# Upper and lower parts of 32 sample rows side by side as one 64-column stationary tile

## The reference

```python
h = rmsnorm(x, g_norm)
p = h @ w_in                                  # 1024 x 1408
u, v, xb, q = ...                             # 384, 384, 384 and 256 columns
a_out = gelu(u) * (causal W_s @ rmsnorm(gelu(v), g_v) + b_s)    # chunked spatial gate
b_out = pooled means of xb minus xb, a linear map per group, times a scale
x_out = attention of q into the memory keys and values
x = x + concat(rmsnorm of a_out, b_out, x_out) @ w_out
```

## Time and profile before

| what | value |
|---|---|
| median of 3 runs | 1500.94 us (1499.5 to 1501.42) |
| the profiled execution | 1504.31 us |
| its span, first to last instruction | 1502.6 us |
| PE busy | 1455.8 us, 97% of the span |
| DVE, ACT, POOL busy | 1175.2, 952.2, 112.2 us |
| HBM traffic | 303 GB/s over the span |
| mean granted TensorE clock | 0.991 of full speed |

### The profile page before, as it was taken

The page is one execution under the profiler, slowest core; times in us unless marked ns, Lnnn a source line. Parts: engine busy times, 40 slices in busy tenths (PEclk is TensorE's granted clock), DMA queues, the critical chain, the costliest instruction groups (busy, mean ns, idle before and its releaser), DMA issues.

```text
span 1502.6 us, 21721 instructions
## 1 busy us (share of the span) xinstructions
PE 1455.8 (97%) x7712; PEld 1239.2 (82%) x7712; DVE 1175.2 (78%) x1113; ACT 952.2 (63%) x914; POOL 112.2 (7%) x132
## 2 busy tenths in 40 slices
PE   7998999999999999999999999999999999999996
PEld 5888999999888778888888888888888887888774
DVE  6546776645546588888888888888888888889996
ACT  7535433344444667777777777777777776777773
POOL 1211311002122200000000000000000000001021
PEclk9999999999999899999999999999999999999998
DMA  9524687655422699999999999999999999999991
GB/s 376 224 91 150 228 273 273 238 180 185 174 86 85 245 367 362 360 395 363 357 390 365 364 383 378 369 367 384 369 353 395 370 360 356 362 371 362 390 384 64
DMA packets 67282, 456.32 MB, mean 304 GB/s; under 512 B 7636, under 2 KB 7930, under 8 KB 15639
## 3 DMA queue, kind: packets, MB, share of 16 engines
q1 hardware_dynamic: 59543, 427.91, 75.1%
q0 software_dynamic: 5680, 20.49, 3.5%
q10 hardware_dynamic: 2016, 7.34, 1.2%
HBM read 434.10 MB, written 21.88 MB: 303 GB/s over the span
## 4 chain that ended last, share of the span: by engine, by line
PE 89%; ACT 3%; DVE 3%; issue 2%; ACTq 0%; POOL 0%; DMA 0%; DVEq 0%; POOLq 0%; SPq 0%
PE bank L321 28%; PE bank L323 28%; PE bank L322 28%; ACT whi L305 2%; PE bank L1800 2%; DVE wlo L309 1%; ACT junk L537 1%; DVE x L1220 1%; PE bank L1553 0%; PE bank L1778 0%; DVE stage L1008 0%; PE bank L1755 0%; ACTq L776 0%; DMA stage<-in_mem 0%; DVE hT_lo L859 0%
## 5 line engine op out<-in xcount | busy, mean ns | idle before, releaser
L309 DVE TENSOR_TENSOR wlo<-raw,whi 128x2048 fp32r<-128x2048 f32 x401 | 918.6, 2291 | 187.8 <-ACT whi L305 186.6
L305 ACT ACTIVATE whi<-raw 128x2048 fp32r<-128x2048 f32 x401 | 767.1, 1914 | 155.4 <-PE bank L323 154.5
L321 PE MATMUL bank<-whi,gT_hi 128*128 128x512 f32 x896 | 364.8, 407 | 3.3 <-DVE gT_lo L1225 3.3
L323 PE MATMUL bank<-whi,gT_lo 128*128 128x512 f32 x896 | 355.5, 397 | 0.0
L322 PE MATMUL bank<-wlo,gT_hi 128*128 128x512 f32 x896 | 354.3, 395 | 0.0
L323 PEld LDWEIGHTS bank<-whi,gT_lo 128*128 128x128 f32 x896 | 169.3, 189 | 39.6
L321 PEld LDWEIGHTS bank<-whi,gT_hi 128*128 128x128 f32 x896 | 169.9, 190 | 37.6 <-issue 3.5
L322 PEld LDWEIGHTS bank<-wlo,gT_hi 128*128 128x128 f32 x896 | 170.1, 190 | 34.7
L321 PE MATMUL bank<-whi,eT_hi 128*128 128x512 f32 x448 | 177.4, 396 | 1.9 <-DVE eT_lo L1240 1.9
L322 PE MATMUL bank<-wlo,eT_hi 128*128 128x512 f32 x448 | 177.1, 395 | 0.0
L323 PE MATMUL bank<-whi,eT_lo 128*128 128x512 f32 x448 | 176.2, 393 | 0.0
(11 more groups left out here) (253 smaller groups left out, 1476.1 us busy)
## 6 DMA issues: line engine op xcount, KB each, us to landing
raw<-in_stream SPq DMA_DIRECT2D x402, 1024.0 KB, 5.6
x_slots<-zero POOLq DMA_DIRECT2D x18, 640.0 KB, 6.4
rows_e<-x_slots ACTq DMA_DIRECT2D x7, 512.0 KB, 7.5
y_slots<-y_rows ACTq DMA_DIRECT2D x7, 512.0 KB, 6.2
const<-in_const SPq DMA_DIRECT2D x1, 1192.0 KB, 21.7
stage<-in_mem SPq DMA_DIRECT2D x2, 512.0 KB, 4.3
xn<-in_x_prompt SPq DMA_DIRECT2D x1, 1024.0 KB, 11.0
out_y_prompt<-xm SPq DMA_DIRECT2D x2, 512.0 KB, 2.6
```

Source lines behind the costliest of these rows:

```text
L305: nc.scalar.activation(whi[:, slot % SPL, :], raw[:, slot, :], ACT.Copy).then_inc(hi_ready, 1)
L309: nc.vector.tensor_tensor(wlo[:, slot % SPL, :], raw[:, slot, :], whi[:, slot % SPL, :].bitcast(F), ALU.subtract).then_inc(lo_ready, 1)
L321: nc.tensor.matmul(out, a_hi, b_hi, start=start, stop=False, **kw)
L323: return nc.tensor.matmul(out, a_lo, b_hi, start=False, stop=stop, **kw)
```

## The change

The two 32-column stationary tiles of the sample rows, hi and lo, become one tile of 64 columns. Block k of `hT_hi` gets 32 more columns, and a copy on DVE (`pack`) puts the sample columns of `hT_lo` there. For t = 2 PE then issues two products in place of three: the 64-column tile by whi and by wlo. Rows 0 to 31 of the bank get hi by (hi + lo), rows 32 to 63 lo by (hi + lo), so that the product lo by lo, left out before, is in the result. The two halves must be added: ACT copies rows 32 to 63 from the bank to SBUF (`pair_low`), DVE adds rows 0 to 31 (`pair_sum`), and the gelu or the scaling reads that sum (`pairs`, in a buffer that is free in this stage).

```diff
-        hT_hi = ph("hT_hi", [P, KD, NT], FR)
+        hT_hi = ph("hT_hi", [P, KD, NT + NS], FR)
...
+            def pair_low(b):
+                nc.scalar.activation(pairs, bank[b][NS:2 * NS, 0:DA], ACT.Copy).then_inc(S["pair_in"], 1)
...
+            def gelu_rows(to, t):
+                src = pairs if t == 2 else bank[t][:, 0:DA]
+                return nc.scalar.activation(to[0:ROWS[t], t, :], src, ACT.Gelu_apprx_tanh,
+                                            scale=rstd[0:ROWS[t], N_MIX, t:t + 1])
...
                 hi_static(act, c0 + 7)
-                for t in range(3):
+                act.wait_ge(rstd_ok, rstd_event(l, E_MIX))
+                for t in range(2):
                     act.wait_ge(S["v_done"], 3 * l + t + 1)
-                    act.wait_ge(rstd_ok, rstd_event(l, E_MIX))
-                    last = nc.scalar.activation(vg[0:ROWS[t], t, :], bank[t][0:ROWS[t], 0:DA], ACT.Gelu_apprx_tanh,
-                                                scale=rstd[0:ROWS[t], N_MIX, t:t + 1])
-                last.then_inc(S["vg_out"], 1)
+                    gelu_rows(vg, t)
+                act.wait_ge(S["v_done"], 3 * l + 3)
+                pair_low(2)
+                act.wait_ge(S["pair_out"], 3 * l + 1)
+                gelu_rows(vg, 2).then_inc(S["vg_out"], 1)
                 act.wait_ge(S["vg_out"], l + 1)
                 sum_squares(vg, N_V)
                 hi_static(act, c0 + 8, c0 + 9)
+                act.wait_ge(S["xb_done"], 3 * l + 3)
+                pair_low(6)
                 act.wait_ge(chunk_used, c0 + 10)
-                for t in range(3):
-                    last = nc.scalar.activation(ug[0:ROWS[t], t, :], bank[t][0:ROWS[t], 0:DA], ACT.Gelu_apprx_tanh,
-                                                scale=rstd[0:ROWS[t], N_MIX, t:t + 1])
-                last.then_inc(S["ug_out"], 1)
+                act.wait_ge(S["xb_out"], l + 1)
+                pair_low(2)
+                for t in range(2):
+                    gelu_rows(ug, t)
+                act.wait_ge(S["pair_out"], 3 * l + 3)
+                gelu_rows(ug, 2).then_inc(S["ug_out"], 1)
                 hi_static(act, c0 + 10)
...
+            def pack(l):
+                dve.wait_ge(hx_lo, times(l, 0) + KD)
+                V.tensor_copy(hT_hi[:, :, NT:NT + NS], hT_lo[:, :, SEQ:NT].bitcast(F)).then_inc(S["hx_packed"], 1)
+            def pair_sum(n, b):
+                dve.wait_ge(S["pair_in"], n)
+                V.tensor_tensor(pairs, pairs, bank[b][0:NS, 0:DA], ALU.add).then_inc(S["pair_out"], 1)
...
                 last.then_inc(S["qs_out"], 1)
+                pack(l)
                 lo_static(dve, c0 + 4)
...
                 link(V.reciprocal(rden[:, :], den[:, :]))
+                pair_sum(3 * l + 1, 2)
                 lo_static(dve, c0 + 8, c0 + 9)
-                for t in range(3):
+                for t in range(2):
                     dve.wait_ge(S["xb_done"], 3 * l + t + 1)
...
+                pair_sum(3 * l + 2, 6)
+                dve.wait_ge(S["pair_out"], 3 * l + 2)
+                V.tensor_scalar(xb[0:NS, 2, :], pairs, rstd[0:NS, N_MIX, 2:3], None, ALU.mult).then_inc(S["xb_out"], 1)
...
                 last.then_inc(S["v_out"], 1)
+                pair_sum(3 * l + 3, 2)
                 for i in range(4):
                     dve.wait_ge(S["PT_done"], 4 * l + i + 1)
...
             def rows_times(c, b, n_blocks, k, banks, first, last_k):
...
-                for t in range(3):
+                for t in range(2):
...
+                both, to = hT_hi[:, k, SEQ:NT + NS], bank[banks + 2][0:2 * NS, 0:n_blocks * P]
+                T.matmul(to, both, blk(whi, c, b, n_blocks), start=first, stop=False)
+                out.append(T.matmul(to, both, blk(wlo, c, b, n_blocks), start=False, stop=last_k))
...
                 arrived(c0 + 5)
+                pe.wait_ge(S["hx_packed"], l + 1)
```

More of the change, by code:

```diff
@@ L155, in build @@
         qs = [t[:, :, :].rearrange("p f c -> p (f c)") for t in (qs_hi, qs_lo)]
-        sPT = [t[:, :, :].rearrange("p k t -> p (k t)") for t in (hT_hi, hT_lo)]
+        sPT = [t[:, :, :].rearrange("p k t -> p (k t)")[:, 0:2 * NREQ * DIAG] for t in (hT_hi, hT_lo)]
+        pairs = sq[:, :, :].rearrange("p a b -> p (a b)")[0:NS, 0:DA]
         mem = stage[:, :, :].rearrange("p a b -> p (a b)")[:, 0:2 * D].rearrange("p (t d) -> p t d", t=2)
@@ L272, in build @@
             "y_hi_out", "y_out", "y_last_out", "scat_done", "x_added", "fin_out",
-            "to_row_out", "from_row_out", "got_added", "zero_set", "xn_blank", "ident_r_out", "xm_blank", "xm_turned", "ticked", "settled")}
+            "to_row_out", "from_row_out", "got_added", "zero_set", "hx_packed", "pair_in", "pair_out", "xn_blank", "ident_r_out", "xm_blank", "xm_turned", "ticked", "settled")}
         zero_filled, x_spread, rows_in, y_saved, got_in = (
@@ L545, in turn_hi @@
                     act.wait_ge(turned, KD * l + k + 1)
-                    nc.scalar.activation(hT_hi[:, k, :], bank[k % 2][:, 0:NT], ACT.Copy,
+                    nc.scalar.activation(hT_hi[:, k, 0:NT], bank[k % 2][:, 0:NT], ACT.Copy,
                                          scale=gains[:, l, G_GROUP, k:k + 1]).then_inc(turned_hi, 1)
@@ L558, in hi_of_x @@
                 for k in blocks:
-                    nc.scalar.activation(hT_hi[:, k, :], xT[:, k, :], ACT.Copy,
+                    nc.scalar.activation(hT_hi[:, k, 0:NT], xT[:, k, :], ACT.Copy,
                                          scale=gains[:, l, which, k:k + 1]).then_inc(hx_hi, 1)
@@ L859, in turn_lo @@
                     V.scalar_tensor_tensor(out=hT_lo[:, k, :], in0=bank[k % 2][:, 0:NT],
-                                           scalar=gains[:, l, G_GROUP, k:k + 1], in1=hT_hi[:, k, :].bitcast(F),
+                                           scalar=gains[:, l, G_GROUP, k:k + 1], in1=hT_hi[:, k, 0:NT].bitcast(F),
                                            op0=ALU.mult, op1=ALU.subtract).then_inc(turned_lo, 1)
@@ L875, in lo_of_x @@
                     V.scalar_tensor_tensor(out=hT_lo[:, k, :], in0=xT[:, k, :], scalar=gains[:, l, which, k:k + 1],
-                                           in1=hT_hi[:, k, :].bitcast(F), op0=ALU.mult, op1=ALU.subtract).then_inc(hx_lo, 1)
+                                           in1=hT_hi[:, k, 0:NT].bitcast(F), op0=ALU.mult, op1=ALU.subtract).then_inc(hx_lo, 1)
+            def pack(l):
[4 more added lines that the diff above has]
+                V.tensor_tensor(pairs, pairs, bank[b][0:NS, 0:DA], ALU.add).then_inc(S["pair_out"], 1)
             def mean_of_x(u, n, b):
@@ L966, in _ @@
                 link(V.reciprocal(rden[:, :], den[:, :]))
+                pair_sum(3 * l + 1, 2)
                 lo_static(dve, c0 + 8, c0 + 9)
-                for t in range(3):
+                for t in range(2):
                     dve.wait_ge(S["xb_done"], 3 * l + t + 1)
-                    last = V.tensor_scalar(xb[0:ROWS[t], t, :], bank[4 + t][0:ROWS[t], 0:DB],
-                                           rstd[0:ROWS[t], N_MIX, t:t + 1], None, ALU.mult)
-                last.then_inc(S["xb_out"], 1)
+                    V.tensor_scalar(xb[0:ROWS[t], t, :], bank[4 + t][0:ROWS[t], 0:DB],
+                                    rstd[0:ROWS[t], N_MIX, t:t + 1], None, ALU.mult)
+                pair_sum(3 * l + 2, 6)
+                dve.wait_ge(S["pair_out"], 3 * l + 2)
+                V.tensor_scalar(xb[0:NS, 2, :], pairs, rstd[0:NS, N_MIX, 2:3], None, ALU.mult).then_inc(S["xb_out"], 1)
                 dve.wait_ge(rstd_ok, rstd_event(l, E_V))
@@ L1465, in queries @@
                         m = mm3(bank[4 + f][:, 0:NT], blk(whi, c0 + 2, 2 * k + f), blk(wlo, c0 + 2, 2 * k + f),
-                                hT_hi[:, k, :], hT_lo[:, k, :], k == 0, k == KD - 1)
+                                hT_hi[:, k, 0:NT], hT_lo[:, k, :], k == 0, k == KD - 1)
                     if k == KD - 1:
@@ L1627, in project @@
                         m = mm3(bank[(2, 3, 4, 5, 6, 7, 0, 1)[d]][:, 0:NT], blk(whi, c, 4 * (k % 4) + d % 4),
-                                blk(wlo, c, 4 * (k % 4) + d % 4), hT_hi[:, k, :], hT_lo[:, k, :], k == 0, k == KD - 1)
+                                blk(wlo, c, 4 * (k % 4) + d % 4), hT_hi[:, k, 0:NT], hT_lo[:, k, :], k == 0, k == KD - 1)
                     return m
@@ L1659, in first_up @@
                     for w in range(2):
-                        m = mm3(bank[2 + w][:, 0:NT], blk(whi, C_UP, 2 * k + w), blk(wlo, C_UP, 2 * k + w), hT_hi[:, k, :],
+                        m = mm3(bank[2 + w][:, 0:NT], blk(whi, C_UP, 2 * k + w), blk(wlo, C_UP, 2 * k + w), hT_hi[:, k, 0:NT],
                                 hT_lo[:, k, :], k == 0, k == KD - 1)
@@ L1669, in route @@
                     pe.wait_ge(hx_lo, times(l, 1) + k + 1)
-                    mm3(bank[2][0:NE, 0:NT], rt_hi[:, k, :], rt_lo[:, k, :], hT_hi[:, k, :], hT_lo[:, k, :], k == 0, False)
```

(3 more changed lines are left out.)

## The result

| | runs | median us | range | ratio to before |
|---|---|---|---|---|
| before | 4 | 1500.22 | 1499.38 to 1501.42 | |
| after | 4 | 1491.24 | 1489.36 to 1492.65 | 0.9938 (0.9925 to 0.995) |
| after, once more (`x2_after_again`) | 5 | 1491.33 | 1490.42 to 1491.86 | 0.9934 (0.9921 to 0.9947) |

The change makes the kernel 9.0 us faster (7.5 to 11.3 by the interval), and 9.6 in the second set (8.0 to 11.9; before 1500.96 there). The row products and their waits behave much as forecast; the rest of the gain comes from a place that the prediction took to be fixed.

The account below looks back on a forecast made before the run. The prediction took PE alone to bound the row products. Removed products (-8.38 us) and the third sums' delay (+1.16) gave -7.22 us, from a median of 1500.94 to 1493.7 us; range 1492.2 to 1496.3.

Parts of the forecast that it names:

- What a product costs: Row products on PE: 174.5 ns from start to start, taken for a product with 64 columns too.
- Gain of 4.19 us in a layer: Row products: 24 fewer in a layer at 174.5 ns, all counting where supply holds; 8.38 us in both layers.
- the table load: ACT's gelu table load before v: if it came behind the wait for v, about 0.1 us lost in each layer.
- Cost of the third sum: End of u: the third pair_sum delays the PT copy ahead of attend; PE loses 0.58 us in a layer, 1.16 in both.
- The supply stall: Row products: PE stalls at c0+5, c0+6, c0+8; 0.5 us a layer gives 1494.7, 1 us 1495.7; chance above 1 us 0.09.
- A wide tile: Row products: 64-column products show their load, 0.19 us from start to start, +1.5 us, 1495.2 us; chance 0.06.
- drain at a change of width: Row products: 64-column products cannot overlap 128-column neighbours, 162 ns per change, +15.6 us, 1509.3 us; chance 0.03.
- given back in the experts: Experts' stage starts no earlier in effect, for instance bound by loads; layer 1's 3.6 us lost, 1497.3 us; chance 0.06.
- The step that failed: From attend of layer 1 on: the rest moves as one, so the sum of -7.22 us carries through to the end.
- two slices with the clock at 8 tenths, not one: Whole span: PE's granted clock was read as 9 tenths or more in all slices but one.
- the formula for the gap between products: Row products: N / 2.4 + 2.5 ns, 162.5 ns here, making the removed products worth 3.9 us in a layer.

Follow-up runs that it names:

- ten-product kernel: The kernel before with one product more (lo by lo) for each block of the sample rows, ten in place of nine: 1510.65 us, ratio 1.0066.
- four idle instructions: The kernel before with four copies of 3 columns added to ACT's list in layer 0, nothing else: 1497.93 us, ratio 0.9989.
- the 124: The changed kernel with 124 semaphore increments that nobody waits for added to ACT's list, 62 in each layer: 1493.93 us, ratio 0.9962.
- pair work: The kernel before's three 32-column products for the sample rows, with all that the change adds on ACT and DVE: 1500.05 us, ratio 0.9998 to before.
- kernel without sums: The changed kernel without the three copies and three sums of the pairs in each layer; products and packing stay: 1491.53 us, ratio 0.9939.
- x1_before_again: The kernel before, unchanged, profiled and timed once more: 1501.28 us, ratio 1.0001.
- x9_late_sum_early_table: The changed kernel with its third pair sum behind two PT copies and ACT's rms wait back behind the wait for v: 1488.56 us, ratio 0.9917.
- x6_late_sum: The changed kernel with its third pair sum moved behind the first two PT copies in DVE's list: 1489.56 us, ratio 0.9924.

## Why the prediction was right and wrong

- **What a product costs: right.** 24 fewer in a layer at 174.5 ns. The ten-product kernel measured 176 ns for one more.
- **Gain of 4.19 us in a layer: 3.7 and 3.6.** The lost 0.5 us is one stall at c0+8 (0.18 us), behind the table load that the text named as a possibility at 0.1 us, the wider starts (0.26 us), and in layer 1 of the first profile 0.1 us at the first product of c0+5.
- **Cost of the third sum: right**, 0.50 us against 0.58. Moving it away gave 0.5 back.
- **Rivals.** The supply stall exists, at 0.2 to 0.3 us in a layer, not 0.5 to 1. A wide tile costs 4 ns, not 15. There is no drain at a change of width: 0.2 us in a layer between wide and narrow. Nothing of the first layers' gain was given back in the experts.
- **The step that failed** is in the sum: "The rest of the kernel, from `attend` of layer 1 on, should move as one, since PE has no gap in the experts and their loads are released by PE and DVE." It did not. ACT's list grew by four instructions, the issue of rows_e moved away from the place where ACT pauses, and it became 2.5 us shorter. In the traces that is 1.5 us of PE's time. The step overlooked that the load of `rows_e` is issued by ACT, and took the length of an issue to be fixed. Without it the gain would have been the 6.4 us of the mixing stages, 1493.8 us, inside the range and next to the forecast.
- **Smaller slips.** The earlier trace rows has two slices with the clock at 8 tenths, not one; nothing was worked out from it. And the formula for the gap between products, 162.5 ns, is called one for a single product by itself in that section of the Trainium skill ("TensorE: Matmul & The Clock Gate"), not one for a stream; the sum went by the 174.5 ns of the trace.
- **Whether that explains all of 9.0 to 9.6.** 6.4 and 1.5 make 7.9, inside the interval of the first set (7.5 to 11.3 us) and at the edge of that of the second (8.0 to 11.9). What the issue alone is worth in the runs is not sharp either: 2.7 us by the four idle instructions and 2.6 by the 124, but 1.5 by the pair work (0.5 faster with 1.0 us more on the path) and 1.6 by the kernel without sums (0.2 slower with 1.4 us less). So 1.1 to 1.7 us stay open. The granted clock of other stretches may hold them, and two differ between the kernels. Here is 1240 to 1285 us of before and of after, first profiles; PE idles about 2 us in it while DVE chooses rows:

```profile
1240.00:1285.00 45.00, 43.04 (x184) 34.49 (x183) 39.28 (x48) 30.28 (x26) 0.00 (x0) 0.96 0.92 359
```

```profile
1240.00:1285.00 45.00, 43.03 (x191) 34.59 (x190) 40.29 (x47) 31.36 (x26) 0.00 (x0) 1.00 0.93 369
```

The 0.96 is 0.90 and 0.76 in the two stretches of 5 us from 1260 to 1270, which makes 3.4 us at 1.2 GHz; the aligned splits show 1.56 us for it. All six profiles with a long issue have 0.96 there, and five of the six with a shorter one have 1.00. If that share held for all runs, it would add 1.3 us to the 1.5. But the profile of the pair work has 1.00 there too, and its runs leave little room for 1.3 us more. That the short issue causes it is argued from twelve profiles and not shown; why it would is open.

The other stretch is the one ahead of the row products of layer 1. There 1.6, 2.9 and 1.4 us went to a low clock in the profiles of `x1_before_again`, `x3_ten_products` and `x5_pair_work_only`, three of the five profiles with nine or ten products in a block, and nothing in the seven with eight. Neither can be told from chance with so few profiles. The profiled execution of before, 3.4 us above its median, holds the 4.6 us ahead of the experts; among the 29 runs of before in the first set of experiments, too, the six of 1503.6 us and more are those with the lowest mean clock, 0.989.

## What to carry to other kernels

A product saved on an engine without gaps is worth its start-to-start distance, read over hundreds of them, and a sum put ahead of a copy on the chain costs its own links; they came out within 4 ns a product and 0.1 us in a layer. "The rest moves as one" is a claim that needs a check of its own: look in the rest for DMA issues on a compute engine's queue that take longer than their like, for instruction packets near them, and count whether the edit changes the number of instructions ahead of them. When an added or removed instruction moves a time far away from it, pad the list with idle ones and see whether the effect follows the count.

## What the runs showed of the hardware

- ACT pauses 0.36 to 0.39 us ahead of its recorded instruction number 505, and ahead of number 633 with 124 more, 128 apart (in `x9_late_sum_early_table` ACT waits for PE at that number, and no pause is to be seen). A packet of 8192 bytes on instruction queue q14 starts 2.1 to 2.6 us after the pause. A DMA issue at most four instructions behind the pause took 3.67 to 3.84 us (six traces), one eight instructions behind it 1.19 to 1.29 us (five), and one ten behind it 0.40 us (one); the first eleven all end 1.56 to 1.62 us after the start of that packet. So the issue ends by the fetch of instructions, and its length tells how early it began. Why it does is not shown. The Trainium skill ("Runtime: NRT & Kernel Launch", section "Instruction fetch mechanics") has an engine's instructions refilled in blocks of 16 KB, 256 instructions, and the crossing of a border mostly hidden. Here the packets of q14 have 8192 bytes, the two pauses are 128 apart, and one crossing costs up to 3.5 us of ACT (3.84 in place of the 0.36 of its other issues) and 1.5 us of PE.
- A change in the order of two waits ahead of an activation decided whether the 1.28 us table load ran before v was ready (67.71 us, `x9_late_sum_early_table`) or waited for it (69.95 us, `x6_late_sum`).
